# Routing stage of a two-layer block: 28 of 80 key columns multiplied in full fp32 instead of as a three-product split

## What is computed

```
q = (hb @ wq).reshape(PEER_BLOCK, PEER_HEADS, 2, PEER_DKEY // 2)
s = jnp.einsum('thsd,snd->thsn', q, subkeys)
s1, i1 = lax.top_k(s[:, :, 0], PEER_TOPK)
s2, i2 = lax.top_k(s[:, :, 1], PEER_TOPK)
cand = s1[..., :, None] + s2[..., None, :]          # 16 x 16 per head
sc, ci = lax.top_k(cand.reshape(..., 256), PEER_TOPK)
idx = i1[ci // 16] * 128 + i2[ci % 16]
gate = softmax(sc)
act = gelu(einsum('td,thkd->thk', hb, u_tab[idx])) * gate
out = einsum('thk,thkd->td', act, v_tab[idx])
```

## Time and profile before

| | |
|---|---|
| median of 3 runs | 3,351.52 us (3,350.27 to 3,356.59) |
| the profiled execution | 3,357.79 us, span 3,356.1 us |
| mean granted TensorE clock | 0.952 of full speed |
| PE busy | 3,086.5 us, 92% |
| PEld busy | 2,574.3 us, 77% |
| DVE busy | 2,430.1 us, 72% |
| ACT busy | 1,762.9 us, 53% |
| routing stage in the span | first key matmul at 541.6 us, last at 892.1 us |

### The profile page before, as it was taken

One profiled execution on the slowest core, in us unless ns is written; L12 is line 12 of the kernel. 1 busy time (PEld: TensorE's weight loads), 2 busy tenths in 40 slices (PEclk: granted clock), 3 DMA queues, 4 the chain that ended last, 5 costly groups with the idle time before them and its releaser, 6 DMA issues. The chain is left out here.

```text
span 3356.1 us, 49912 instructions
## 1 busy us (share of the span) xinstructions
PE 3086.5 (92%) x17008; PEld 2574.3 (77%) x17009; DVE 2430.1 (72%) x3665; ACT 1762.9 (53%) x2206; POOL 39.8 (1%) x47
## 2 busy tenths in 40 slices
PE   7999898889899999977979986879999999999997
PEld 3797546888788999965859866758888888888886
DVE  3665654899788666658645467559889888988986
ACT  3344303436533444435224344248887887888886
POOL 0000000000000000000000000000000000000000
PEclk9998798999999999988989987979999999999999
DMA  7561133345577666631135240169999999999994
GB/s 276 201 226 35 72 135 116 130 148 182 220 250 220 218 212 212 201 115 46 51 129 181 103 155 1 57 232 390 374 357 377 367 360 367 373 363 351 387 366 173
DMA packets 225998, 732.47 MB, mean 218 GB/s; under 512 B 23543, under 2 KB 59816, under 8 KB 223016
## 3 DMA queue, kind: packets, MB, share of 16 engines
q1 hardware_dynamic: 221928, 702.85, 57.2%
q0 software_dynamic: 2768, 23.59, 2.4%
q10 hardware_dynamic: 1152, 4.19, 0.3%
HBM read 702.76 MB, written 28.84 MB: 218 GB/s over the span
## 5 line engine op out<-in xcount | busy, mean ns | idle before, releaser
L3351 DVE TENSOR_TENSOR moe_lo<-moe_raw,moe_hi 128x1024 fp32r<-128x1024 f32 x756 | 886.1, 1220 | 66.5 <-ACT moe_hi L3201 42.7
L3201 ACT ACTIVATE moe_hi<-moe_raw 128x1024 fp32r<-128x1024 f32 x756 | 789.6, 1061 | 151.7 <-PE moe_pB L3149 83.1
L3149 PE MATMUL moe_pB<-moe_hi,moe_hEh 128*128 128x512 f32 x1008 | 399.9, 397 | 2.6 <-DVE moe_hEl L3346 2.6
L3149 PE MATMUL moe_pB<-moe_hi,moe_hEl 128*128 128x512 f32 x1008 | 394.2, 391 | 0.0
L3149 PE MATMUL moe_pB<-moe_lo,moe_hEh 128*128 128x512 f32 x1008 | 393.6, 390 | 0.0
L1547 PE MATMUL route_pS<-fh,route_uh 128*128 128x256 f32 x640 | 191.2, 299 | 36.0 <-DVE route_ul L1650 35.7
L3149 PEld LDWEIGHTS moe_pB<-moe_hi,moe_hEh 128*128 128x128 f32 x1008 | 190.0, 189 | 40.5 <-issue 2.8
L3149 PEld LDWEIGHTS moe_pB<-moe_hi,moe_hEl 128*128 128x128 f32 x1008 | 189.7, 188 | 40.7
L3149 PEld LDWEIGHTS moe_pB<-moe_lo,moe_hEh 128*128 128x128 f32 x1008 | 190.3, 189 | 38.0
L1882 PE MATMUL exp_pO<-exp_vh,exp_ah 128*128 128x512 f32 x512 | 201.1, 393 | 4.2 <-DVE exp_al L1941 4.2
L1882 PE MATMUL exp_pO<-exp_vl,exp_ah 128*128 128x512 f32 x512 | 200.6, 392 | 0.0
(11 more groups left out here) (752 smaller groups left out, 6784.5 us busy)
## 6 DMA issues: line engine op xcount, KB each, us to landing
moe_raw<-in_moe_w SPq DMA_DIRECT2D x758, 512.0 KB, 6.0
exp_vs<-in_peer_v SPq DMA_DIRECT2D x128, 512.0 KB, 4.4
route_us<-in_peer_u SPq DMA_DIRECT2D x64, 512.0 KB, 3.5
exp_us<-in_peer_u SPq DMA_DIRECT2D x64, 512.0 KB, 4.8
inp_w<-in_w_mod SPq DMA_DIRECT2D x48, 512.0 KB, 6.2
inp_w<-in_w_tiles SPq DMA_DIRECT2D x40, 512.0 KB, 6.1
gates<-route_big POOLq DMA_DIRECT2D x8, 2048.0 KB, 8.8
exp_gs<-gates SPq DMA_DIRECT2D x32, 512.0 KB, 5.6
```

The costliest lines, as they stand in the source:

```text
L3149: i = pe.matmul(pB[:, kind], l[:, kd], m[:, n % HALVES, ns], start=kd == 0 and x == 0, stop=kd == KD - 1 and x == 2)
L3201: act.activation(hi[:, n % HALVES], raw[:, n % RING], ACT.Copy).then_inc(hi_ready, 1)
L3351: dve.tensor_tensor(lo[:, n % HALVES], raw[:, n % RING], hi[:, n % HALVES], ALU.subtract).then_inc(lo_ready, 1)
```

## The change

28 columns are taken out of the split (`WHOLE`): 26 to 33, 51 to 58, and of the 20 columns from 60 on those whose number modulo 5 (counted from 60) is 0, 2 or 4, so 60, 62, 64, 65, 67, 69, 70, 72, 74, 75, 77, 79. For these ScalarE makes no `uh` and VectorE no `ul`; TensorE waits for the load itself and multiplies `us` with `fT`, both fp32, in 8 matmuls. SyncE reloads such a slot when TensorE has ended the column (`s_psum`), and not when VectorE has subtracted. The 52 that stay split are counted on their own (`NUMBER`), for the semaphores and the two buffers. This is the whole diff:

```diff
--- before.py
+++ after.py
@@ -1486,6 +1486,11 @@
     LAST = (PART + 2 + 24 - 1, PART + 2 + 24 + 1 + 24 - 1)
     FREE = COLUMNS - LAST[1] - 2
 
+    WHOLE = {first + n for first in (PART + 2, LAST[0] + 2) for n in range(16, 24)}
+    WHOLE |= {LAST[1] + 2 + n for n in range(FREE) if n % 5 in (0, 2, 4)}
+    SPLIT = [n for n in range(COLUMNS) if n not in WHOLE]
+    NUMBER = {n: m for m, n in enumerate(SPLIT)}
+
     def with_group(g):
         return (g + 1) * FREE // GROUPS_ > g * FREE // GROUPS_
 
@@ -1520,8 +1525,10 @@
             @block.sync
             def _(sp):
                 def load(n):
-                    if n >= RING:
-                        sp.wait_ge(ul_ready, n - RING + 1)
+                    if n - RING in WHOLE:
+                        sp.wait_ge(s_psum, n - RING + 1)
+                    elif n >= RING:
+                        sp.wait_ge(ul_ready, NUMBER[n - RING] + 1)
                     sp.dma_start(us[:, n % RING], wq[n] if n < NQ else u[n - NQ]).then_inc(u_loaded[n % RING], 16)
                 load(0)
                 load(1)
@@ -1539,11 +1546,18 @@
             @block.tensor
             def _(pe):
                 def scores(n):
-                    pe.wait_ge(ul_ready, n + 1)
+                    if n in WHOLE:
+                        pe.wait_ge(u_loaded[n % RING], (n // RING + 1) * 16)
+                    else:
+                        pe.wait_ge(ul_ready, NUMBER[n] + 1)
                     if n >= 2:
                         pe.wait_ge(s_out, n - 1)
                     for kd in range(KD):
-                        for q, (w, x) in enumerate(((uh[:, n % 2, kd], fh), (uh[:, n % 2, kd], fl), (ul[:, n % 2, kd], fh))):
+                        if n in WHOLE:
+                            m = pe.matmul(pS[:, n % 2, 0:T], us[:, n % RING, kd], fT[:, kd], start=kd == 0, stop=kd == KD - 1)
+                            continue
+                        half = NUMBER[n] % 2
+                        for q, (w, x) in enumerate(((uh[:, half, kd], fh), (uh[:, half, kd], fl), (ul[:, half, kd], fh))):
                             m = pe.matmul(pS[:, n % 2, 0:T], w, x[:, kd], start=kd == 0 and q == 0, stop=kd == KD - 1 and q == 2)
                     m.then_inc(s_psum, 1)
 
@@ -1592,10 +1606,12 @@
                 act.activation(fh[:], fT[:], ACT.Copy).then_inc(fh_ready, 1)
 
                 def keys(n):
+                    if n in WHOLE:
+                        return
                     act.wait_ge(u_loaded[n % RING], (n // RING + 1) * 16)
-                    if n >= 2:
-                        act.wait_ge(s_psum, n - 1)
-                    act.activation(uh[:, n % 2], us[:, n % RING], ACT.Copy).then_inc(uh_ready, 1)
+                    if NUMBER[n] >= 2:
+                        act.wait_ge(s_psum, SPLIT[NUMBER[n] - 2] + 1)
+                    act.activation(uh[:, NUMBER[n] % 2], us[:, n % RING], ACT.Copy).then_inc(uh_ready, 1)
 
                 def out(n):
                     act.wait_ge(s_psum, n + 1)
@@ -1646,8 +1662,10 @@
                 dve.tensor_tensor(fl[:], fT[:], fh[:], ALU.subtract).then_inc(f_ready, 1)
 
                 def column(n):
-                    dve.wait_ge(uh_ready, n + 1)
-                    dve.tensor_tensor(ul[:, n % 2], us[:, n % RING], uh[:, n % 2], ALU.subtract).then_inc(ul_ready, 1)
+                    if n in WHOLE:
+                        return
+                    dve.wait_ge(uh_ready, NUMBER[n] + 1)
+                    dve.tensor_tensor(ul[:, NUMBER[n] % 2], us[:, n % RING], uh[:, NUMBER[n] % 2], ALU.subtract).then_inc(ul_ready, 1)
 
                 def first_best(values, top, rows):
                     for r in rows:
```

## The result

The changed kernel takes 3,328.47 us (median of 4 runs, 3,325.15 to 3,331.40), the kernel before in the same comparison 3,350.89 us (4 runs, 3,347.69 to 3,356.59). The ratio is 0.9931, with a 95% interval from 0.9914 to 0.9948: 22.4 us faster, with an interval of some 17 to 29 us. The forecast was 3,330 us in a range of 3,325 to 3,343.

The account below looks back on a forecast made before the run. VectorE was taken to set the time where the 16 best are chosen and the gate tables made. Gains of 9.5 (first half), 9.7 (second half) and 2.4 us (tables), 21.6 in all, gave 3,330 us from 3,351.5, range 3,325 to 3,343.

Parts of the forecast that it names:

- VectorE's share: In each half of the choice, eight subtractions fewer on VectorE make the gates ready 8.64 us earlier.
- The late turn: TensorE transposes the choices without waiting for a subtraction, so VectorE's idle of 1.27 and 1.21 us before the turns goes.
- X: TensorE's time for one whole column, 8 full fp32 matmuls: 3.57 us, between 3.42 and 3.75, against 2.96 us split.
- B: Rival: whole columns cost about what they save; at X = 4.5, 0.7 us in all, no change; chance 0.04.
- C: Rival: a whole column's 16 matmul records don't overlap, so it takes 6.06 us; kernel slower, 3,395 us; chance 0.03.
- The tables: In the gate tables the pace passes from VectorE to TensorE: 126.5 us against 128.9, a gain of 2.4 us.
- D: Rival: TensorE sets the pace throughout, so 28 x 0.61 = 17 us are added; 3,369 us; chance 0.02.
- rival A: Tables gain 0.2 us or nothing, and idle before the turns lowers TensorE's clock; 3,336 us; chance 0.16.
- The first is a third of that: Argument against rival A: TensorE's idle before the first turn, some 1 us, against some 3 us before the second.
- A's other clock term: After the second turn, some 1.4 us of low clock would not be hidden by the tables' first wait.

Follow-up runs that it names:

- Run 3: The changed kernel with the last column of each half (33 and 58) split again; 3,328.13 us, executed once.
- run 4: The changed kernel with all 24 columns from 35 to 58 whole instead of 8; 3,334.24 us, executed once.
- run 6: The changed kernel with all 20 columns of the gate tables whole instead of 12; 3,327.43 us, executed once.
- run 5: The changed kernel with 8 instead of 12 whole columns in the gate tables; 3,321.36 us, executed once.
- run 8: The changed kernel rebalanced: whole are columns 25 to 33, 49 to 58 and 8 of 20 in the tables; 3,324.27 us, ratio 0.9916 to the kernel before.
- run 10: The balanced version (whole: 25 to 33, 49 to 58, 8 in the tables) repeated in the changed kernel's rounds; 3,319.99 us, ratio 0.9911 to the kernel before.

## Why the prediction was right, and where it was not

- **VectorE's share.** 8.64 us were forecast for eight subtractions. From the first maximum to the gates it was 94.68 us and is 86.15 us: 8.53 us. Right in sum: at 1.14 us each it would have been 9.12 us. Which of the eight gave back less was not looked at.
- **The late turn.** VectorE's idle of 1.27 and 1.21 us went to zero in both halves. The path forecast, column 34 one subtraction after the gates, came to 654.00 us, which is 660.67 in times of before (660.6 forecast). That low clock stood behind the late turn is in the trace before: the granted clock from 664.3 to 669.6 us, where column 33 ran, is 0.50. Run 3 shows the same at column 58, and that its size is not fixed.
- **The price of a whole column.** X was taken at 3.57 us between 3.42 and 3.75, and is 3.45: the records are 0.216 us apart (0.217 forecast), and the 0.1 us of handoff does not exist between whole columns. This decides against B and C. It is also less than the 3.95 us estimated from the four passes for true fp32 of the Trainium skill ("FP8 and Floating Point Precision", TensorE Precision Notes) against the three products of the split: a fp32r matmul of 256 elements starts 0.12 us after the last, so three of them take 0.36 us, where the two records of a full one take 0.432 us, 1.2 times and not 4/3.
- **The tables.** 2.35 us against 2.4, but by two errors that cancel. X was 0.12 us too high, 12 x 0.12 = 1.4 us for the better. The products were put at 1.70 and 1.73 us for 16 records and take up to 1.79 us where fp32 follows (a whole column, or the next group's products): 8 groups take 791.41 - 761.01 = 30.4 us by TensorE's timeline (30.3 forecast), of which 3 x 3.45 + 2 x 2.96 are columns, so the products are 14.1 us and not 13.7, 1.7 us for the worse over the stage. That the gain came out to 0.05 us is luck. VectorE waited 7.9 us for TensorE in the 32 groups, 2.0 us in 8, where about 3 us were forecast.
- **TensorE as the bound.** That D's 17 us didn't come, while run 4 and run 6 each turned slower than with fewer whole columns, is one and the same finding: the engine that sets the pace changes from stretch to stretch. The rule of the Trainium skill ("Perfetto Trace Analysis", Identifying the Most-Contended Engine) to start with the engine of the highest occupancy holds within a stretch, and over the span, where TensorE led before by matmuls (92%) and by weight loads (77%) against VectorE's 72%, it points the wrong way for this edit.
- **The clock (rival A), the step that was judged badly.** "The first is a third of that" was given as the reason why an idle gap of 1 us before the first turn would not bring the clock down, and A got 0.16. The gap was 1.94 us, since the whole columns were cheaper than forecast, and low clock at column 34 came in five of the seven traces that have this gap. The first trace of the change was one of the other two, and that the sum met it to 0.1 us is luck. A's other clock term, 1.4 us of the second half not hidden by the tables, was nothing: low clock after the second turn came every time and cost nothing. The gain in the timed runs was 22.4 us in the first comparison (17 to 29) and 18.3 us in the second (15 to 24). Low clock that costs 1.2 to 2.7 us would put the gain at 18.9 to 20.4 us, between the two, but the intervals overlap, and timed runs carry no such rows: that it is the cause of the difference is not shown.

Not tried was a version that fills the idle before the turn with other work at no other change; that the gap brings the clock down rests on seven traces with it and three with 0.6 to 0.7 us (runs 3, 8 and 10), in which the clock stayed up after the first turn. Why it fell in five of the seven and not in the other two stays open.

## What to carry to other kernels

Where a costlier form on one engine relieves another, cut the stage into stretches and give the costly form only to those in which its engine waits, in as many pieces as it has idle time for; near the best number a few pieces more or less decide little (none, 8, 12 and 20 pieces here: 129.0, 126.1, 126.7 and 131.3 us), but idle that is left before dependent work on TensorE can cost its clock. Take the price of a new shape from the distance of starts in long chains of its neighbours, not from durations or a single short group. And measure such an edit between points of the trace inside its stage, since what lies before it moves by more than the gain of a part.

## What was not expected of the hardware

- An idle gap of 1.94 us on TensorE, three transposes and another 0.59 us of waiting were enough to bring the granted clock from 2.4 to 1.2 GHz in five of seven traces of the same code at that place. The low stretch then lasted from 2.6 to 6.2 us, though TensorE was busy without a gap in it. A gap of 2.77 us once did not bring it down (run 3). The gap of 3.7 us before the second turn was followed by low clock in six traces of six.
- Handoffs between matmuls depend on the neighbours: 16 product records take 1.70 us before a column of float32r and 1.79 us before a full fp32 one (1.79 us in the tables of the change, 1.70 us in those of the kernel before and of run 5), while between two fp32 columns nothing is added to 0.216 us.
